# Another order of weight loads, row buffers, routing steps and group norms around a gather loop

## The reference

```python
def first_block(x, mem, ...):
    h = x
    h = h + hybrid_mixer(rms_norm(h, norm_mix), ...)
    h = h + memory_cross_attention(rms_norm(h, norm_x), rms_norm(mem, norm_mem), ...)
    h = h + peer_ffn(rms_norm(h, norm_ffn), ...)   # per token and head: 16 experts by score;
    return rms_norm(h, norm_final)                 # sum of gate * gelu(x . u) * v over them

# second_block, first layer: h = _rms(x, norm_g) * (1 + sc) + sh, then _conv_mixer:
#   a, b, g = split(h @ w_in, 3);  y = a * sigmoid(b);  31-tap convolution, layernorm, silu(g), @ w_out
# second layer: the same norm and modulation, then _pool_mixer
```

## Time and profile before

| | us |
|---|---|
| median of 3 runs | 1162.19 (1161.01 to 1163.0) |
| the profiled execution | 1163.75 |
| its span, first to last instruction | 1161.9 |
| PE, DVE, ACT, POOL busy in the span | 922.7, 782.8, 367.3, 320.4 |
| last gather issued, its data landed | 942.2, 958.1 |

### The profile page before, as it was taken

How to read it: one execution, slowest core, us unless ns; L and a number is a source line. 1 busy time by engine, 2 the same in 40 slices (tenths; PEclk the granted TensorE clock), 3 DMA queues, 4 the chain that set the end, 5 groups by cost and what they waited for, 6 DMA issues and landing times. The chain is left out here.

```text
span 1161.9 us, 19635 instructions
## 1 busy us (share of the span) xinstructions
PE 922.7 (79%) x7714; PEld 720.6 (62%) x7714; DVE 782.8 (67%) x2079; ACT 367.3 (32%) x912; POOL 320.4 (28%) x284
## 2 busy tenths in 40 slices
PE   6999999887687796778234457898977657999998
PEld 6998697875576484566112135785654314988887
DVE  4766645787898776855378978787786664953411
ACT  2511111235322222312011131685683108543100
POOL 0001000234334342523245444444454420000000
PEclk9999899989899698888555567999899577999999
DMA  9987596999999999999999999999999986343101
GB/s 356 424 347 305 223 402 251 381 421 424 382 421 421 421 416 423 421 422 422 424 421 421 421 420 420 419 402 421 417 371 421 422 358 269 143 186 110 73 1 37
DMA packets 51853, 402.65 MB, mean 347 GB/s; under 512 B 5809, under 2 KB 8369, under 8 KB 9393
## 3 DMA queue, kind: packets, MB, share of 16 engines
q0 software_dynamic: 40320, 293.62, 61.5%
q1 hardware_dynamic: 10432, 105.61, 22.4%
q10 hardware_dynamic: 1008, 2.16, 0.5%
HBM read 400.32 MB, written 1.05 MB: 345 GB/s over the span
## 5 line engine op out<-in xcount | busy, mean ns | idle before, releaser
L482 POOL DMA_INDIRECT arena<-uv_dram,arena x194 | 233.7, 1205 | 345.9 <-PE ps L679 277.2
L1778 DVE CUSTOM_DVE_ANT_0 arena<-arena 128x1024 f32<-128x1024 f32 x194 | 234.7, 1223 | 91.9 <-DMA arena<-uv_dram,arena 88.7
L679 PE MATMUL ps<-arena 128*32 128x256 f32 x1552 | 132.4, 470 | 167.2 <-DVE arena L1814 166.8
L679 PEld LDWEIGHTS ps<-arena 128*32 128x32 f32 x1552 | 47.0, 125 | 237.4 <-DVE arena L1814 201.1
L1225 ACT ACTIVATE gel<-dots 128x2 f32<-128x2 f32 x128 | 26.0, 203 | 399.2 <-DVE dots L1778 378.2
L536 PEld LDWEIGHTS ps<-xn,wring 128*128 128x128 f32 x896 | 107.9, 201 | 6.5 <-issue 6.3
L536 PE MATMUL ps<-xn,wring 128*128 128x128 f32 x896 | 111.1, 286 | 0.0
L482 POOL DMA_INDIRECT wring<-uv_dram,arena x62 | 73.6, 1187 | 102.0 <-PE ps L679 92.6
L1778 DVE CUSTOM_DVE_ANT_0 wring<-wring,arena 128x1024 f32<-128x1024 f32 x62 | 75.2, 1223 | 35.5 <-DMA wring<-uv_dram,arena 34.8
L1814 DVE TENSOR_SCALAR arena<-const,gel,arena 128x32 f32<-128x32 f32 x256 | 65.9, 313 | 27.4 <-ACT gel L1225 22.1
L679 PE MATMUL ps<-wring,arena 128*32 128x256 f32 x496 | 44.0, 486 | 49.0 <-DVE arena L1814 49.0
(11 more groups left out here) (319 smaller groups left out, 1553.6 us busy)
## 6 DMA issues: line engine op xcount, KB each, us to landing
wring<-units_dram SPq DMA_DIRECT2D x39, 2048.0 KB, 11.6
arena<-mod_dram POOLq DMA_DIRECT2D x24, 1024.0 KB, 9.2
arena<-units_dram SPq DMA_DIRECT2D x8, 2048.0 KB, 8.7
arena<-uv_dram,arena POOLq DMA_INDIRECT x194, 14.1
wring<-units_dram SPq DMA_DIRECT2D x2, 1024.0 KB, 8.3
hA<-x_t_dram SPq DMA_DIRECT2D x2, 512.0 KB, 7.7
arena<-mem_t_dram SPq DMA_DIRECT2D x1, 1024.0 KB, 9.8
arena<-keys_dram ACTq DMA_DIRECT2D x2, 512.0 KB, 6.8
```

Of the source, the lines that this page charges most:

```text
L482: pool.indirect_dma_start(row(n), None, uv_d, bass.IndirectOffsetOnAxis(ap=idx[:, n:n + 1], axis=0)).then_inc(sem(f"row_in{b}"), 16)
L679: mm = pe.matmul(acc_ps(q)[G * c:G * (c + 1), :], lhsT=diag[:, s % 2, j, :], rhs=row(n)[:, D + 256 * c:D + 256 * (c + 1)], start=(p == 0 a ...
L1778: post(V.tensor_tensor_reduce(out=row(n)[:, 0:D], in0=row(n)[:, 0:D], in1=x_rep[q % 2], scale=1.0, scalar=0.0, op0=ALU.mult, op1=ALU.add, ...
```

## The change

- **Loads.** Unit `b` of tile 1 moves ahead of `q`, `v` and `k` in `LOADS` and goes to slot 5, the `arena` columns 0 to 4095, which are also row buffers 0 and 1. The units behind it alternate between slots 0 and 1 as before, one place earlier.
- **Row buffers.** Until `b` has been multiplied, rows can't use buffers 0 and 1. `FIRST_PLACES` puts rows 0 to 13 into six buffers (2 to 5 and two at columns 12288 and 14336), rows 14 and 15 into 6 and 7. So row n waits for row n - 6 for n from 6 to 13, rows 4 and 5 wait for unit `pq1` of tile 0, and row 16 waits for unit `b` of tile 1.
- **Routing.** The 112 steps up to slot 45 are spread otherwise: 20 steps in slots 5 to 10 (15 before), none in slots 11 to 14 (9 before), the rest later.
- **Group norms.** For the three groups that are normed inside the slots (not tile 0), the 8 small DVE operations on 128x32 and the 8 ACT shifts become three DVE operations on all blocks (`group_normed`), and the 8 of `h3_final` become two in one slot (`group_final`).
- **Sigmoid.** Group 4's products, sigmoid and gating run one slot earlier, so its tanh is in slot 103 and the roots of the next group stay in slot 104.

```diff
-LOADS[_n:_n + 3] = [(1, "q"), (1, "v"), (1, "k")]
+LOADS[_n:_n + 4] = [(1, "b"), (1, "q"), (1, "v"), (1, "k")]
...
+B_SLOT = 5
...
-LOAD_SLOT = ([i % 3 for i in range(len(CHAIN_UNITS[0]) - 1)] + [PQ1_SLOT, 0, 1, 2] + [i % 2 for i in range(len(CHAIN_UNITS[1]) - 3)]
+LOAD_SLOT = ([i % 3 for i in range(len(CHAIN_UNITS[0]) - 1)] + [PQ1_SLOT, B_SLOT, 0, 1, 2] + [i % 2 for i in range(len(CHAIN_UNITS[1]) - 4)]
...
+FIRST_PLACES = [2, 3, 4, 5, 8, 9, 2, 3, 4, 5, 8, 9, 2, 3, 6, 7]
+BEFORE_ROW = {**{n: n - 6 for n in range(6, 14)}, 18: 12, 19: 13, 20: 8, 21: 9}
...
-    _upto = 4 * _s if _s < 5 else 16 + -(-(_s - 4) * 96 // 41)
+    _upto = 4 * _s if _s < 5 else 16 + -(-(min(_s, 10) - 4) * 20 // 6) if _s < 15 else 36 + -(-(_s - 14) * 76 // 31)
...
-TOKEN_SLOTS = {4: (95, 1), 5: (107, 1), 6: (123, 2)}
+TOKEN_SLOTS = {4: (94, 1), 5: (107, 1), 6: (123, 2)}
...
-                if n >= RING:
-                    pool.wait_ge(sem(f"row_free{b}"), n // RING)
-                if n == 6:
+                if n >= 6:
+                    before = BEFORE_ROW.get(n, n - RING)
+                    pool.wait_ge(sem(f"row_free{before % RING}"), before // RING + 1)
+                if n == 4:
                     pool.wait_ge(sem("pairs"), PAIR_NO[0, "pq1"] + 1)
-                if n == RING + 6:
+                if n == 14:
                     pool.wait_ge(sem("pairs"), PAIR_NO[1, "k"] + 1)
+                if n == 16:
+                    pool.wait_ge(sem("pairs"), PAIR_NO[1, "b"] + 1)
...
+            def group_normed(part):
+                n = H3_PARTS[part]
+                x = xn[:, :, n]
+                go(V.tensor_tensor(x, hA[:, :, n], each_token(gain_both[:]), ALU.mult))
+                need(dve, "h3_root", part + 1)
+                go(V.tensor_tensor(x, x, each_block(both[:, :, n]), ALU.mult))
+                go(V.tensor_tensor(x, x, each_token(modc[:, 0:KB]), ALU.add), "shifted0")
+
+            def group_final(part):
+                h = hA[:, :, H3_PARTS[part]]
+                go(V.tensor_tensor(h, h, each_token(col("norm_final", 0, KB)), ALU.mult))
+                go(V.tensor_tensor(h, h, each_block(rms[:, :, H3_PARTS[part]]), ALU.mult))
```

More of the change, by code:

```diff
@@ L242, in build @@
         ring = [area(2048 * b, 2048) for b in range(6)] + [wring[:, 2, 4 * i:4 * i + 4, :].rearrange("p k n -> p (k n)") for i in range(2)]
+        places = ring + [area(12288, 2048), area(14336, 2048)]
         def row(n):
-            return area(12288 + 2048 * (n - 6), 2048) if n in (6, 7) else ring[n % RING]
+            return places[FIRST_PLACES[n] if n < len(FIRST_PLACES) else n % RING]
         mem_n = blocks(area(0, 2048), KB)
@@ L1207, in slot @@
                         h3_roots(part)
[L1208 to L1211, removed]
+                    if p in (10, 11) and part == 0:
+                        h3_shift(part, p - 10)
                 if s >= AB_SLOT + 3 and (s - AB_SLOT - 3) % 2 == 0 and (s - AB_SLOT - 3) // 2 < KB:
@@ L1729, in h3_final, with each_token, each_block @@
                 go(ins)
+            def each_token(ap):
+                return ap.unsqueeze(2).broadcast_to([P, KB, G])
+            def each_block(ap):
+                return ap.broadcast_to([P, KB, G])
+            def group_normed(part):
[9 more added lines that the diff above has]
+                go(V.tensor_tensor(h, h, each_block(rms[:, :, H3_PARTS[part]]), ALU.mult))
             def glu_half(b):
@@ L1789, in slot @@
                     part = H3_GROUPS.index(q)
[L1790 to L1794, removed]
+                    if p in (9, 10) and part == 0:
+                        h3_normed(part, p - 9)
+                    if p in (11, 12) and part == 0:
                         h3_final(part, p - 11)
+                    if p == 9 and part:
+                        group_normed(part)
+                    if p == 11 and part:
+                        group_final(part)
                 if s == PER_TILE + 2:
@@ L2179, in _ @@
             group_done(GROUPS - 1)
[L2181 to L2185, removed]
             n = H3_PARTS[4]
```

## The result

The changed kernel takes 1168.88 us (median of five runs, 1167.73 to 1168.99), the kernel before 1161.65 on the same chip: so the two medians are 7.2 us apart. The ratio over all runs is 1.0069, with a 95% interval of 1.0056 to 1.0082; that is 8.0 us slower, between 6.5 and 9.5. The forecast was +8.8 us and a median of 1171.0.

A forecast was written before the change was run, and what follows sets the result against it. The prediction took the DMA engines as the bound: bytes over 421 GB/s plus idle time. Its terms, 13.6 - 2.7 - 2.1 = +8.8 us on 1162.2, gave 1171.0 us, range 1163.5 to 1176.5.

The forecast's parts named there:

- What bounds the kernel: First to last gather: time is bytes over 421 GB/s plus DMA idle time; only idle between 206 and 958 us counts.
- The wait of row 16: Row 16 and those behind it wait for unit `b`, so the DMA engines idle from 281.6 to 295.2, 13.6 us.
- Bytes: Seven units and rows 0 to 15, 31.5 MB, are all that can be issued before row 16, landed by about 281.6.
- `b`'s delay: `b` ends at 291.0 instead of 285.0: 5.0 us for later rows, 0.5 each for routing in slots 5 and 6.
- The restart: After row 16's wait, some 4.2 us pass before data move: soonest landing 6.7 us, of which 2.5 are bytes.
- The early load: Unit `b` goes out at 204.9, ahead of the first rows; its 5.0 us of transfer delay slot 0 by 5.0 us.
- Routing: Slots 11 to 14 lose 9 steps and the gap at 310 to 324 us goes, -2.7 us, also without the edit.
- My third rival: Exp moved to slot 7 adds a 1.28 us table load; DMA runs dry again by 2 to 5 us: 1175; chance 0.11.
- Sigmoid: Tanh moved to slot 103: slot 104 ends 2.1 us sooner, taking -2.1 of the 3.4 us lost at 844 to 868.
- the 2.6 that I gave as a sign: In slot 104, two table loads on ACT and a wait of about 2.6 us would show the forecast.
- Norms: Fewer group norm operations: DVE gains 0.7 us per group for three groups; effect 0, at best -1.3 us.
- Same: Idle time stays at 8.6 because DVE sets slots 0 to 7, later gaps close: +1.2 to +2.3, some 1164 us; chance 0.08.

The follow-up runs named there:

- e9: The kernel before plus one line: POOL waits for the end of tile 1's unit `b` before issuing row 16; 1167.27 us, ratio 1.0070.
- e2: The kernel before with only the early load of `b`, its slot, the six row buffers and the waits; 1171.46 us, ratio 1.0089.
- e10: The kernel before with only the six buffers for rows 0 to 13, `b` loaded where it was, no wait of row 16; 1160.38 us, ratio 1.0001.
- e1: The changed kernel with loads, row buffers and POOL waits as before; routing, norms and sigmoid stay changed; 1161.15 us, ratio 1.0008.
- e6: e1 with routing as before up to slot 11, none in slots 12 to 14, the gates' Exp back in slot 8; 1159.39 us, ratio 0.9992.
- e4: The changed kernel with group 4's products, sigmoid and gating back in their old slots, tanh in slot 104; 1167.03 us, ratio 1.0056.
- e5: The changed kernel with rows 16 to 19 in free buffers, later buffers reused in that turn, row 20 waiting for `b`; 1165.52 us, ratio 1.0047.
- e7: The kernel before with tile 1's unit `q` loaded ahead of tile 0's `pq1`, in the idle time before 206 us; 1159.36 us, ratio 0.9993.

## Why the prediction was right, and where its terms were off

**What bounds the kernel** held: the chain enters the last stretch through the last gather, and what the DMA engines lose between the load of `pq1` and that landing adds up, within 0.6 us, to how much later it comes (table under *The sum*).

**The wait of row 16** was the term that decides, and e9 shows that this wait alone, in the kernel before, costs as much as the whole change (1.0070 against 1.0069). Its sum was 291.0 - 281.6 + 4.2 = 13.6, and 10.8 came out. Counted from the load of `pq1`:

| | forecast | measured |
|---|---|---|
| queue dry | 281.6 - 204.5 = 77.1 | 278.7 - 201.7 = 77.0 |
| end of `b`, before 80.5 | +6.0 | 84.7, +4.2 |
| end of `b` to data again | 4.2 | 289.5 - 286.4 = 3.1 |
| pause | 13.6 | 10.8 |

- *Bytes* were right to 0.1 us.
- *`b`'s delay* was sized 1.8 us too high. The term for the later rows was right: row 1's dot product starts 12.8 us after row 0's issue in the earlier trace rows and 17.9 now (235.23 - 217.37), and `b` ends 84.6 us after the load of `pq1` in e2 against 79.7 in e10, which has neither the early load nor the changed routing; the first half of `b` took 3.84 us in both. The 1.0 us for routing was the term that failed: the changed kernel's 84.7 is only 0.1 above e2, so DVE's two more steps hardly delayed `b`. The last 0.8 us are the clock of one execution: in the trace that I priced from, the first half of `b` took 5.47 us, and its end at 80.5 is 0.8 behind that of e10. 4.9 + 0.1 - 0.8 is the 4.2 of the table.
- *The restart* was sized 1.1 us too high. I took what a landing takes beyond its bytes, 4.2 us, for the time before data move. From row 16's issue at 287.24 it is 2.2 us to data, 0.8 more lies ahead of it on POOL. The least landing of the earlier trace rows holds something that isn't dead time at the start. The Trainium skill ("DMA: Bandwidth & Descriptors", "Anatomy of one DMA - SWDGE (gpsimd) path") has 2.0 us fixed, but puts most of it behind the last byte. Here 2.2 us lie ahead of the first data, so this trace doesn't bear out that share. An estimate that takes the page's 2.0 for the whole restart would have given a pause of about 11.4 us.

**The early load.** I had counted its 5 us only as a delay of `b`. But its bytes also keep the queue alive 5 us longer: it runs dry 71.5 us after the load of `pq1` in e9 and 77.0 in the changed kernel, while `b` ends at 80.6 and 84.7. The 1.4 us that this gives are lost again at the restart. It takes 1.4 us from the end of `b` in e9, where SP's load of `h` also waits for `b`, and 3.1 in the changed kernel. So the pause is 10.5 us without the preload and 10.8 with it. My sum held both, in different terms, and so I didn't see that the preload hardly changes the pause. The times of e2 (1.0089) and e9 (1.0070) leave room for 2 us between them, but their intervals overlap. e10 bears out that the six buffers cost nothing.

**Routing.** The forecast for the whole edit was -2.7 us, "also without the edit". The second half is right: in e9 the gap closes with the routing of before. The edit itself loses 3.7 us near 310 us when no pause ahead of it has filled the queue (e1 against e6). My third rival named that table load and asked for 2 to 5 us on top of the pause. The table load is there (DVE's wait for the roots is 4.8 us in the changed kernel, 3.4 before), but the eight rows issued at once behind it cover it, and no second dry stretch came.

**Sigmoid.** The mechanism held, and its size rested on one trace. I wrote that the wait of DVE would fall by 2.1 us; the six traces with the new order against e4 show 2.2. The rest of the 4.7 us was a wait of ACT for PE behind a dip of the clock, so the wait left in slot 104 is 0.25 us and not the 2.6 that I gave as a sign. What the move saves of the transfers is 3.4 us between the two profiled executions, but 0.6 to 3.5 in six traces with the old order, 1.6 in the mean. I had read the size of a gap in one trace as a property of the kernel; e4's times don't show the gain at all.

**Norms**: 0 us, and nothing in e1 against before speaks against that, though no run has them alone. The operations took what I said: three of 0.41 to 0.43 us, and two of 0.42.

**The sum.** What the DMA engines lose, in us, in stretches counted from the load of `pq1`, as length x (1 - rate/421):

| stretch | before | changed | e1 | e2 | e6 | e9 |
|---|---|---|---|---|---|---|
| 70 to 95, the pause | -0.1 | 11.6 | -0.1 | 11.4 | 0.1 | 10.7 |
| 95 to 125, near 310 us | 2.8 | -0.1 | 6.1 | -0.1 | 2.4 | 0.0 |
| 540 to 600 | 1.3 | 2.6 | 1.6 | 3.4 | 1.6 | 1.7 |
| 635 to 680, behind slot 104 | 3.5 | 0.1 | 0.0 | 1.6 | 0.0 | 1.0 |
| 720 to the last landing | 3.8 | 4.8 | 4.8 | 3.4 | 4.6 | 5.3 |
| last landing | 753.5 | 761.9 | 754.8 | 762.5 | 751.3 | 761.3 |

From before to changed that is +11.7 - 2.9 - 3.4 = 5.4 us for the three terms of the forecast (13.6 - 2.7 - 2.1 = 8.8). Another 1.3 and 1.0 us come from two stretches for which the forecast has no term, and 0.6 from none of these. So the total was close by luck: the pause was sized 2 to 3 us too high, the gain behind slot 104 was 1.3 too low for this pair of traces, and 2.9 us of loss elsewhere made up for both. The 11.6 us of the first row are more than the pause of 10.8, since the stretch also holds short windows of lower rate on both sides of it.

**The rivals.** *Same* was given 0.08 for a short pause because DVE sets slots 0 to 7; half of that is true. What I missed is its other side: between 220 and 324 us the transfers and the slots are both near their limit. So e5 and e7, which free the DMA engines, get back a third of what they free or less.

Open: why the landing of the last gather comes 5.1 us after the rate falls in the changed kernel and 3.9 before. The larger loss at 770 to 786 us doesn't come from the norms: in the same stretch, 540 to 600, the norms of before stand with 3.4 us in e2 and 2.9 in e10, and the changed ones with 1.3 in e5.

## What to carry to other kernels

Before a resource is put to a second use, ask what in-order queue will wait for its release, and compare two numbers: the bytes issued ahead of that wait, over the rate, and the time at which the releasing product ends. Here they were 71.5 and 80.6 us with the wait alone (e9). The preload of 5 us of bytes ahead of it made them 77.0 and 84.7: it moved both, and the pause stayed. A gap in one trace should be sized from several: the one that was 3.5 us here was 0.6 to 2.1 in five others with the same order.

## What the runs showed of the hardware

- After a dry queue data moved as if at the full rate from 2.2 us after a gather's issue, though no gather landed in under 6.7 us. A load by SP restarted the queue sooner: in e9 `h` can go out when `b` ends at 281.9, and data flow as if from 283.3, 0.6 us after row 16 was issued at 282.7.
- The same code in tile 0 got a granted clock from 120 to 140 us that differed between executions, and with it all that follows. At 1.00 (six traces) the load of `pq1` is issued at 200.8 to 201.7 us, at 0.91 (three) at 202.6 to 203.5, and at 0.83 (three) at 204.5 to 204.8. Later dips stand at other places in each trace: from 832 to 836 us the kernel before has 0.50 and the changed one 1.00.
